# MLP down projection: a new order of products, and low parts of four weight loads a job by a turned copy and an adding transfer

## The reference

```python
        u = jax.nn.relu(rms_norm(h, mlp_norm_g) @ w_up)
        h = h + (u * u) @ w_down
```

## Time and profile before

| | |
|---|---|
| device time, median of 3 runs | 2504.21 us (2503.29 to 2504.7) |
| span of the profiled execution | 2504.0 us |
| granted TensorE clock, mean | 0.997 |
| busy: TensorE, VectorE, ScalarE, GpSimd | 2480.6, 1753.6, 1257.8, 29.5 us |
| down projection (L957 to L959) | 3 x 434 matmuls |

### The profile page before, as it was taken

The page is one execution under the profiler, slowest core; times in us unless marked ns, Lnnn a source line. Parts: engine busy times, 40 slices in busy tenths (PEclk is TensorE's granted clock), DMA queues, the critical chain, the costliest instruction groups (busy, mean ns, idle before and its releaser), DMA issues.

```text
span 2504.0 us, 38061 instructions
## 1 busy us (share of the span) xinstructions
PE 2480.6 (99%) x15416; PEld 2115.6 (84%) x15416; DVE 1753.6 (70%) x1978; ACT 1257.8 (50%) x1506; POOL 29.5 (1%) x26
## 2 busy tenths in 40 slices
PE   9999999999999999999999999999999999999998
PEld 7888888888888888888888888888888888888886
DVE  6656765668668677675777777775776666777777
ACT  7655344544444444445555555544654444444543
POOL 0000000000000000000000000000000000000000
PEclk9999999999999999999999999999999999999999
DMA  9454545546546546555545454556465565556553
GB/s 381 153 183 152 176 153 193 176 164 223 193 161 231 187 171 211 193 195 183 185 153 185 153 185 153 185 170 195 150 217 185 186 200 187 183 194 198 186 188 127
DMA packets 128239, 465.97 MB, mean 186 GB/s; under 512 B 14368, under 2 KB 14624, under 8 KB 127168
## 3 DMA queue, kind: packets, MB, share of 16 engines
q1 hardware_dynamic: 127920, 463.53, 55.2%
q10 hardware_dynamic: 144, 0.02, 0.0%
HBM read 461.39 MB, written 2.10 MB: 185 GB/s over the span
## 4 chain that ended last, share of the span: by engine, by line
PE 94%; issue 4%; DVE 2%; ACT 0%; DMA 0%; SPq 0%; DVEq 0%; POOL 0%; POOLq 0%
PE job L970 30%; PE job L982 16%; PE job L938 11%; PE job L940 11%; PE job L939 11%; PE job L957 2%; PE job L958 2%; PE job L959 2%; PE att L958 2%; PE att L957 2%; PE att L959 2%; PE att L1177 1%; PE att L998 0%; DVE w_low L1593 0%; PE att L1010 0%
## 5 line engine op out<-in xcount | busy, mean ns | idle before, releaser
L1274 ACT ACTIVATE w_high<-raw 128x1024 fp32r<-128x1024 f32 (+1 forms) x883 | 919.6, 1050 | 733.9 <-PE job L940 292.4
L1593 DVE TENSOR_TENSOR w_low<-raw,w_high 128x1024 fp32r<-128x1024 f32 (+1 forms) x883 | 1047.0, 1212 | 310.5 <-ACT w_high L1274 231.0
L970 PE MATMUL job<-actA,w_high 128*128 128x512 f32 x3328 | 798.3, 391 | 0.1
L970 PEld LDWEIGHTS job<-actA,w_high 128*128 128x128 f32 x3328 | 611.8, 188 | 119.9 <-issue 0.7
L982 PEld LDWEIGHTS job<-actA,w_low 128*128 128x128 f32 x3328 | 426.7, 191 | 16.2
L982 PE MATMUL job<-actA,w_low 128*128 128x256 f32 x3328 | 431.7, 283 | 0.0
L1796 DVE TENSOR_TENSOR slots<-job,slots 128x512 f32<-128x512 f32 x102 | 70.5, 691 | 344.1 <-ACT slots L1466 343.5
L938 PE MATMUL job<-w_high,actB 128*128 128x512 f32 x736 | 288.6, 392 | 2.5 <-DVE w_low L1593 2.0
L939 PE MATMUL job<-w_low,actB 128*128 128x512 f32 x736 | 287.1, 390 | 0.0
L940 PE MATMUL job<-w_high,actB 128*128 128x512 f32 x736 | 287.0, 390 | 0.0
L938 PE MATMUL job<-w_high,actA 128*128 128x512 f32 x576 | 230.9, 401 | 0.0
(11 more groups left out here) (257 smaller groups left out, 1906.0 us busy)
## 6 DMA issues: line engine op xcount, KB each, us to landing
raw<-in_weights SPq DMA_DIRECT2D x855, 512.0 KB, 4.2
M<-in_mem_t SPq DMA_DIRECT2D x8, 256.0 KB, 8.0
slots<-in_mem SPq DMA_DIRECT2D x2, 1024.0 KB, 12.2
M<-in_x_t SPq DMA_DIRECT2D x4, 512.0 KB, 13.8
H<-in_x SPq DMA_DIRECT2D x2, 1024.0 KB, 9.0
out<-H SPq DMA_DIRECT2D x8, 256.0 KB, 3.2
slots<-in_w_small SPq DMA_DIRECT2D x1, 1024.0 KB, 9.7
slots<-in_post_mix_g SPq DMA_DIRECT2D x1, 1024.0 KB, 4.3
```

The lines of the kernel that those rows point to most:

```text
L970: mm = nc.tensor.matmul(J[job.buf][:, x, :], w_high[:, w % AHEAD, cols], act_both[job.act][:, c, :, :].rearrange("p a t -> p (a t)"), star ...
L1274: nc.scalar.activation(w_high[:, s % AHEAD, cols], raw[:, s % RAW_SLOTS, cols], ACT.Copy)\
L1593: nc.vector.tensor_tensor(w_low[:, s % AHEAD, cols], raw[:, s % RAW_SLOTS, cols], w_high[:, s % AHEAD, cols].bitcast(F32), ALU.subtract).t ...
```

## The change

- The order of the pairs becomes eight 2, eight 3, seven 0, "dma" 4, seven 1, "dma" 5, eight 6, eight 7. A "dma" pair has the same windows and products as an eight.
- In a "dma" window VectorE makes no low part. ScalarE writes `w_low = -raw`, rounded as `w_high` is, by a second copy with scale -1, and GpSimd issues a transfer that adds `raw` to `w_low`. TensorE waits for its landing (one semaphore per slot), as does SyncE before it loads over that `raw`.
- Waits that counted low parts by windows count by those that VectorE makes (`LOWS`), and landings by slot.
- The C banks are numbered the other way round, so that `add_quads` is two instructions of 1024 columns in place of four of 512, and two adds of `add_sevens` become one.
- The forms are addressed by job of `u`; here they are as before those of job 0.

```diff
-QUAD_ORDER = (("eight", 2), ("seven", 0), ("eight", 3), ("eight", 4), ("seven", 1), ("eight", 5), ("eight", 6), ("eight", 7))
+QUAD_ORDER = (("eight", 2), ("eight", 3), ("seven", 0), ("dma", 4), ("seven", 1), ("dma", 5), ("eight", 6), ("eight", 7))
...
+def by_dma(w):
+
+    job, k = WINDOW[w]
+    return job.kind == "quads" and job.parts[k][0] == "dma"
...
+LOWS = list(itertools.accumulate(int(not by_dma(w)) for w in range(PLAN.windows)))
+DMA_LOWS = list(itertools.accumulate(int(by_dma(w)) for w in range(PLAN.windows)))
+
+SLOT_DMA_LOWS = [sum(map(by_dma, range(w % AHEAD, w + 1, AHEAD))) for w in range(PLAN.windows)]
...
+        def low_made(engine, w):
+
+            if by_dma(w):
+                engine.wait_ge(rest_landed[w % AHEAD], 16 * SLOT_DMA_LOWS[w])
+            else:
+                engine.wait_ge(low_ready, LOWS[w])
...
             if what == "C":
-                return J[buf][:, x[0], :] if i == 0 else att[:, 2 * buf + x[0], :]
+                return J[buf][:, i, :] if x[0] == 0 else att[:, 2 * buf + i, :]
...
-                    sp.wait_ge(low_ready, w - RAW_SLOTS + 1 + (part_of(w - RAW_SLOTS) == 0))
+                    low_made(sp, w - RAW_SLOTS + (part_of(w - RAW_SLOTS) == 0))
...
+            def split(w, s):
+                if by_dma(s):
+                    pool.wait_ge(negated, DMA_LOWS[s])
+                    nc.gpsimd.dma_start(w_low[:, s % AHEAD, :].bitcast(F32), raw[:, s % RAW_SLOTS, :],
+                                        accum_op=ALU.add).then_inc(rest_landed[s % AHEAD], 16)
+
+            walk(n, lambda w: None, split, stage)
...
                 first_of(w)
-                pe.wait_ge(low_ready, w + 1)
+                if by_dma(w):
+                    pe.wait_ge(high_ready, w + 1)
+                low_made(pe, w)
...
                     .then_inc(high_ready, 1)
+                if by_dma(s):
+
+                    nc.scalar.activation(w_low[:, s % AHEAD, :], raw[:, s % RAW_SLOTS, :], ACT.Copy, scale=-1.0)\
+                        .then_inc(negated, 1)
...
                     return
+                if by_dma(s):
+                    return
                 if part_of(s) == 1:
                     sums_of(s)
...
-                dve.wait_ge(low_ready, s + 3 - RAW_SLOTS)
+                low_made(dve, s + 1 - RAW_SLOTS)
+                low_made(dve, s + 2 - RAW_SLOTS)
...
-                    nc.vector.scalar_tensor_tensor(hh(1, 0), u_two, r1, hh(1, 0), ALU.mult, ALU.add)
-                    done(nc.vector.scalar_tensor_tensor(hh(1, 1), u_two, r1, hh(1, 1), ALU.mult, ALU.add))
+                    both = hh(1, 0, 2).rearrange("p (i n) -> p i n", i=2)
+                    done(nc.vector.scalar_tensor_tensor(both, u_two.unsqueeze(1).to_broadcast([P, 2, COLS]), r1, both,
+                                                        ALU.mult, ALU.add))
...
-                    for i in range(2):
-                        for t in range(TT):
-                            hh = H[:, t, (c + i) * COLS:(c + i + 1) * COLS]
-                            ins = nc.vector.scalar_tensor_tensor(hh, quad_bank(buf, ("C", i, t)), rstd2[:, t:t + 1], hh,
-                                                                 ALU.mult, ALU.add)
+                    for t, banks in enumerate((J[buf][:, :, :], att[:, 2 * buf:2 * buf + 2, :])):
+                        hh = H[:, t, c * COLS:(c + 2) * COLS].rearrange("p (i n) -> p i n", i=2)
+                        ins = nc.vector.scalar_tensor_tensor(hh, banks, rstd2[:, t:t + 1], hh, ALU.mult, ALU.add)
```

More of the change, by code:

```diff
@@ L60 @@
 MEM_SET, X_SET, MLP_SET, PREMIX_SET, PREFFN_SET = range(5)
-QUAD_ORDER = (("eight", 2), ("seven", 0), ("eight", 3), ("eight", 4), ("seven", 1), ("eight", 5), ("eight", 6), ("eight", 7))
+QUAD_ORDER = (("eight", 2), ("eight", 3), ("seven", 0), ("dma", 4), ("seven", 1), ("dma", 5), ("eight", 6), ("eight", 7))
 SEVENS = [p for what, p in QUAD_ORDER if what == "seven"]
+FORM_JOBS = sorted({p // 2 for p in SEVENS})
 O_EVENT = {2: 1, 3: 2, 0: 3, 1: 4}
@@ L120, in products @@
         what, p, i = self.parts[k]
-        if what == "eight":
+        if what != "seven":
             return [(("C", i, x), ("u", 2 * p + cc, x), cc) for cc in range(2) for x in range(TT)]
@@ L350, in plan_mlp @@
             p.put(job.end + 1, "u_split", j)
-            if j == 0:
-                p.put(job.end + 2, "u_forms", b)
+            if j in FORM_JOBS:
+                p.put(job.end + 2, "u_forms", j)
         paired = (0, 2) if b < FF_BLOCKS - 1 else (0,)
@@ L620, in build @@
         act_high, act_low = ({n: act_both[n][:, :, part, :] for n in "AB"} for part in (0, 1))
-        forms_both = sb("forms_both", [P, 2, 1024], F32R)
+        forms_both = sb("forms_both", [P, 2, 4 * len(SEVENS) * P], F32R)
         H = sb("H", [P, TT, D])
@@ L690, in build, with forms_of @@
         post_g = a2(6)
-        forms, forms_high, forms_low = m_slot(0), forms_both[:, 0, :], forms_both[:, 1, :]
-        form_at = lambda f, p: slice(((f - 1) * 2 + SEVENS.index(p)) * P, ((f - 1) * 2 + SEVENS.index(p) + 1) * P)
+        forms, forms_high, forms_low = Mf[:, 0:4 * len(SEVENS) * P], forms_both[:, 0, :], forms_both[:, 1, :]
+        form_at = lambda f, p: slice(((f - 1) * len(SEVENS) + SEVENS.index(p)) * P,
+                                     ((f - 1) * len(SEVENS) + SEVENS.index(p) + 1) * P)
+        def forms_of(ap, j):
+            mine = [SEVENS.index(p) for p in SEVENS if p // 2 == j]
+            return ap.rearrange("p (f q t) -> p f q t", f=4, t=P)[:, :, mine[0]:mine[-1] + 1, :]
         p1, u_one, u_two = slots[:, 4, 0:COLS], slots[:, 4, COLS:2 * COLS], slots[:, 5, 0:COLS]
@@ L722, in build @@
         sums_made = sem("sums_made")
+        negated, rest_landed = sem("negated"), [sem(f"rest_landed{i}") for i in range(AHEAD)]
         out_ready, half_done, wide_done = sem("out_ready"), sem("half_done"), sem("wide_done")
@@ L853, in stage @@
                                             ALU.pow).then_inc(S["rstd"], 1)
-            walk(n, lambda w: None, lambda w, s: None, stage)
+            def split(w, s):
[4 more added lines that the diff above has]
+            walk(n, lambda w: None, split, stage)
         @block.tensor
@@ L928, in products @@
                 if w > 0:
-                    pe.wait_ge(low_ready, w + 1)
+                    pe.wait_ge(low_ready, LOWS[w])
                 for cc, c in enumerate(chunks_of(w)):
@@ L953, in quads @@
                     else:
-                        once("forms_low", job.needs[1] + 1)
+                        once("forms_low", len(FORM_JOBS) * job.needs[1] + FORM_JOBS.index(where // 2) + 1)
                         ah, al = (a[:, form_at(i, where)] for a in (forms_high, forms_low))
@@ L1268, in split @@
                 if s >= AHEAD and WINDOW[s - AHEAD][0].kind == "features":
-                    act.wait_ge(low_ready, s - AHEAD + 1)
+                    act.wait_ge(low_ready, LOWS[s - AHEAD])
                     act.wait_ge(wide_done, WIDE[s - AHEAD])
@@ L1475, in stage @@
                     wait(act, n, "h_added", 0)
-                    nc.scalar.activation(forms_high, forms, ACT.Copy).then_inc(S["forms_high"], 1)
+                    nc.scalar.activation(forms_of(forms_high, a[0]), forms_of(forms, a[0]), ACT.Copy).then_inc(S["forms_high"], 1)
                 elif name == "add_sevens":
@@ L1889, in stage @@
                     wait(dve, n, "forms_high", 0)
-                    u = a_slot(2).rearrange("p (q c x t) -> p q c x t", q=2, c=2, x=TT)
+                    j, to = a[0], forms_of(forms, a[0])
+                    u = a_slot(2 + j % 2).rearrange("p (q c x t) -> p q c x t", q=2, c=2, x=TT)
+                    u = u[:, [p % 2 for p in SEVENS if p // 2 == j][0]:[p % 2 for p in SEVENS if p // 2 == j][-1] + 1]
                     a11, a12, a21, a22 = (u[:, :, c, x, :] for x, c in ((0, 0), (0, 1), (1, 0), (1, 1)))
-                    s1, s2, s3, s4 = (forms[:, i * T:(i + 1) * T].rearrange("p (q t) -> p q t", q=2) for i in range(4))
+                    s1, s2, s3, s4 = (to[:, i] for i in range(4))
                     done(nc.vector.tensor_tensor(s1, a21, a22, ALU.add))
@@ L1898, in stage @@
                     wait(dve, n, "forms_high")
-                    nc.vector.tensor_tensor(forms_low, forms, forms_high.bitcast(F32), ALU.subtract)\
+                    nc.vector.tensor_tensor(forms_of(forms_low, j), to, forms_of(forms_high, j).bitcast(F32), ALU.subtract)\
                         .then_inc(S["forms_low"], 1)
```

## The result

The changed kernel takes 2573.05 us (median of 4 runs, 2572.66 to 2573.5) against 2504.45 for the kernel before beside it: a ratio of 1.0274 (95% interval 1.0259 to 1.0288), **68.6 us slower**. The forecast was 2558.1, slower, with a range of 2514 to 2596.

A forecast was written before the change was run, and what follows sets the result against it. The prediction took TensorE, busy 99% of the span, to bound the kernel. From 2504.2 us, less 6.3 for the order, plus 37.8 for transfer stalls and 22.4 for the clock, it forecast 2558.1 us, range 2514 to 2596.

The forecast's parts named there:

- the 6.3 us: Down projection, first down job of each block: the new order removes two stalls, 4 x 1.57 us gained.
- The lead: Before windows 8 and 14: 4.76 us of matmuls less 2.36 of copies and hops leaves 2.4 us for the transfer.
- L: Adding transfer's time from issue to landing: 5.0 us taken, between 3.1 and 6.8, giving 14 stalls, 37.8 us in all.
- quiet 1024 KB load: Transfer of 1024 KB on a quiet queue in the earlier trace, 4.3 us, taken as nearest to the adding transfer.
- the lower estimate: Windows 8 and 14, by the Trainium skill's fit of 3.2 us for a 512 KB GpSimd transfer: 14 x 0.9 = 12.6 us.
- point (1): SyncE's queue: loads waiting for the adding transfers' landings are still in time, costed at nothing; 10 us if loads take 6.8.
- The bound of 6.8: Longest 512 KB weight load in the earlier trace, one behind others; upper end for the adding transfer's time, in us.
- The clock: TensorE's clock falls to its lower level behind each stall at windows 8 and 14: 14 x 1.6 = 22.4 us.
- The sum: Whole kernel: 2504.2 - 6.3 + 37.8 + 22.4 = 2558.1 us.
- Covered: Rival: adding transfer lands within 2.4 us, windows 8 and 14 wait for nothing, 2497.9 us; chance 0.06.
- Clock up: Two rivals, windows 8 and 14 stall without clock falls: short transfer 2509.1 to 2521.7 us, chance 0.10; middle to 2560.9, 0.17.
- Long transfer: Rival: slow GpSimd descriptors, or rings shared with loads so windows 9 and 15 stall too; 2600 us at 8.0; chance 0.16.

The follow-up runs named there:

- e1: Changed kernel with only the new order: pairs 4 and 5 plain eights, no turned copy or adding transfer; 2497.16 us, ratio 0.9975 to the kernel before.
- e2: Changed kernel with pair 4 a plain eight, so only pair 5 goes by adding transfer; 2561.17 us, ratio 1.0233 to the kernel before.
- e6: Changed kernel, only pair 5 by adding transfer, SyncE holding loads of window 16 and later until window 14's transfer landed; 2552.16 us, ratio 1.0194.
- e8: Changed kernel with the transfer a plain copy of raw into w_low, without adding, same queue and places; 2561.57 us, ratio 1.0229.
- e4: Changed kernel with 9 and 16 zero-operand matmuls ahead of TensorE's waits at windows 8 and 14; 2563.22 us, ratio 1.0237.
- e7: Changed kernel with adding transfers only for pair 5, at windows 10 and 11, behind seven 0 and eight 4; 2500.71 us, ratio 0.9988.
- e3: Changed kernel with pairs 4 and 5 plain eights and adding transfers for pairs 6 and 7, windows 16 to 19; 2540.13 us, ratio 1.0144.

## Why the prediction was right, and where it was off

- **What bounds, and the 6.3 us.** Right. The stalls at the first seven go with the new order, 6.3 us (e1).
- **The lead.** Right in kind and nearly in size: the stall is L less 2.1 us at nearly every place (e2, e6 and after), for a forecast of 2.4. The step that was short is the hop to GpSimd: ScalarE's turned copy ended at 560.73 + 1.04 = 561.77, the issue began at 562.09, 0.3 us for my 0.05.
- **L at window 8.** 4.6 us for 5.0, nearer to the quiet 1024 KB load of the earlier trace rows (4.3). Adding costs 1.7 us over a copy (e8); the lower estimate that the prediction sets beside its sum (14 x 0.9) has the size of the plain copy, not of the adding transfer. With the shorter lead the stall came out at 2.5 for a forecast of 2.6: two errors that cancel, so that this term is right is in part luck.
- **L at window 14.** The mis-sized term: 7.1 us in the mean for 5.0, so 35.5 us of stall where 7 x 2.7 = 18.9 stood. The step that failed is one price of L for both places, together with point (1) of what was costed at nothing. There I asked whether loads come late for ScalarE; they do not. I did not ask which loads stand ahead of the adding transfer itself: those that the low parts of the seven release, and they go first. The bound of 6.8 in the earlier trace rows, the load that stood behind others, was the row for that place.
- **My first account of that** (loads released by window 8's landing) fell in e2: without pair 4 it is worse, 8.9 us. The burst belongs to the end of a seven, where VectorE writes several low parts in a row; e2's packets and e6 together show that the loads ahead are the cause.
- **The clock.** 22.4 us forecast as 14 falls of 1.6. Measured 21.0, but otherwise spread: 4.9 behind window 8, where the clock fell after three of the seven stalls of 2.5 us, and 16.1 behind window 14, where it fell after every stall (3.7 us and longer). These are ten falls of 2.1 us in the mean, not 14 of 1.6: that the totals agree is luck. That idle time is the cause is shown by e4.
- **The sum.** -6.6 + 17.8 + 35.5 + 22.9 = 69.6 for the forecast's -6.3 + 37.8 + 22.4 = 53.9; the medians differ by 68.6. The 15 us between forecast and result are window 14's transfers.
- **The rivals.** "Covered" needed a transfer under 2.4 us; even the plain copy took 2.9. "Clock up" held for four of seven stalls at window 8. "Long transfer" came true at one of the two places, by loads ahead and not by GpSimd's own work: e6 leaves that work as it was, and the transfer is short. That windows 9 and 15 stall as well came true only in little, up to 0.4 us at window 9.

Left open: why the packets of GpSimd's queue wait until the loads issued ahead are nearly done instead of taking turns with them, and why 2.5 us of standing still brought the clock down at three places and not at four others.

## What to carry to other kernels

Before a step is given to a transfer, count the time from when its slot is free to when its result is wanted, in matmuls, and set it against the copies, the hops and the transfer one after the other; idle engines count for nothing in that sum. Take the transfer's time from the queue as it is at that place: here the loads issued ahead on another queue went first, so a quiet place with eights ahead (e7) costs nearly nothing where the end of a burst costs 7 us a job. And try the parts of a change one by one: here the order is the gain, and the transfers that came with it cost twelve times as much (74.9 us against 6.3).

## What the runs showed of the hardware

- An adding transfer of 512 KB from SBUF to SBUF on GpSimd's queue took 4.5 to 4.8 us on a quiet queue, a plain copy 2.9 to 3.1; issuing kept GpSimd 0.87 and 0.54 us.
- With loads of SyncE's queue ahead, GpSimd's transfer had no packet on the engines until they were nearly done: 5.0 to 5.3 us after its issue in e2, for 1.4 to 1.6 on a quiet queue (e6).
- VectorE's work (the sums and low parts of these windows) left a transfer's time on a quiet queue as it was: 5.7 to 5.9 us with VectorE at work, 5.8 to 6.0 with VectorE still.
- The clock fell to its lower level (1.2 of 2.4 GHz) after three of seven stalls of TensorE of 2.5 us, and after all of 3.7 us and more in the changed kernel; after none of the seven of 0.8 to 1.0 us at window 8 in e8, and after all seven of 3.9 to 4.9 in e3. With the stalls filled by matmuls on zeros it fell only behind the two longest waits left over (2.6 and 2.8 us of idle time, e4).
